# Attention in a hybrid decoder trunk: the products of probabilities and values issued in four bursts a group instead of eight calls in eight steps

## What is computed

```
q, k_c, v_c, k_s, v_s, k_w, v_w, g = split(rms_norm(x) @ w_in)     # 16 heads of 64, in 4 groups of 4 heads
o_c = softmax(q @ kc.T * scale, causal over blocks) @ vc           # compressed keys and values
o_s = softmax(q @ ks.T * scale, causal) @ vs                       # all 8 selected blocks of 64: the whole sequence
o_w = softmax(q @ kw.T * scale, causal) @ vw                       # a window of 512
o   = gates[0] * o_c + gates[1] * o_s + gates[2] * o_w
x   = x + o @ w_out
```

## Time and profile before

| what | before |
|---|---|
| median of three runs | 1432.88 us |
| the profiled execution's own time | 1434.92 us |
| its span on the core | 1433.1 us |
| TensorE busy | 1416.5 us, 99% |
| VectorE, ScalarE, GpSimd busy | 980.5, 699.4, 253.3 us |
| granted TensorE clock | 0.999 of full |
| the attention stream | from about 83 to 337 us of the span |

### The profile page before, as it was taken

The page is one execution under the profiler, slowest core; times in us unless marked ns, Lnnn a source line. Parts: engine busy times, 40 slices in busy tenths (PEclk is TensorE's granted clock), DMA queues, the critical chain, the costliest instruction groups (busy, mean ns, idle before and its releaser), DMA issues.

```text
span 1433.1 us, 18980 instructions
## 1 busy us (share of the span) xinstructions
PE 1416.5 (99%) x7282; PEld 1165.9 (81%) x7282; DVE 980.5 (68%) x1289; ACT 699.4 (49%) x1116; POOL 253.3 (18%) x278
## 2 busy tenths in 40 slices
PE   8999999999999999999999999999999999999999
PEld 7878888778888888888888877777788888888887
DVE  4797877875697888433487756779544988887231
ACT  5566666654445446422233357778324455455121
POOL 4324334101200000000100008776203000000000
PEclk9999999999999999999999999999999999999999
DMA  8200010311332332232232233332222432221322
GB/s 334 102 30 31 30 60 2 118 60 66 107 122 91 116 118 88 89 116 90 89 118 88 88 120 119 117 118 89 88 89 88 147 118 104 91 95 64 118 91 86
DMA packets 27461, 139.51 MB, mean 97 GB/s; under 512 B 2672, under 2 KB 3440, under 8 KB 17136
## 3 DMA queue, kind: packets, MB, share of 16 engines
q1 hardware_dynamic: 24640, 127.54, 25.5%
q10 hardware_dynamic: 2736, 10.81, 2.1%
HBM read 136.18 MB, written 2.16 MB: 97 GB/s over the span
## 4 chain that ended last, share of the span: by engine, by line
PE 91%; DVE 3%; ACT 3%; POOL 1%; issue 1%; DMA 0%; SPq 0%; ACTq 0%; DVEq 0%; POOLq 0%
PE ps L631 16%; PE ps L633 16%; PE ps L632 16%; PE ps L789 7%; PE ps L787 7%; PE ps L788 7%; PE ps L1045 5%; PE ps L1229 3%; PE ps L1023 2%; PE ps L1003 2%; PE ps L1281 1%; PE ps L768 1%; PE ps L912 1%; PE ps L947 1%; PE ps L948 1%
## 5 line engine op out<-in xcount | busy, mean ns | idle before, releaser
L1870 DVE TENSOR_TENSOR wl<-wraw,wh 128x2048 fp32r<-128x2048 f32 x77 | 176.6, 2294 | 159.6 <-ACT wh L1326 159.6
L1326 ACT ACTIVATE wh<-wraw 128x2048 fp32r<-128x2048 f32 x77 | 147.1, 1911 | 174.4 <-PE ps L633 172.0
L787 PE MATMUL ps<-wh,mix_hi 128*128 128x512 f32 x448 | 174.4, 389 | 0.0
L789 PE MATMUL ps<-wh,mix_lo 128*128 128x512 f32 x448 | 174.3, 389 | 0.0
L788 PE MATMUL ps<-wl,mix_hi 128*128 128x512 f32 x448 | 174.3, 389 | 0.0
L631 PE MATMUL ps<-xh,wh 128*128 128x512 f32 x384 | 152.4, 397 | 0.0
L633 PE MATMUL ps<-xh,wl 128*128 128x512 f32 x384 | 149.7, 390 | 0.0
L632 PE MATMUL ps<-xl,wh 128*128 128x512 f32 x384 | 149.6, 390 | 0.0
L631 PE MATMUL ps<-hidden_hi,wh 128*128 128x512 f32 x352 | 139.4, 396 | 0.0
L633 PE MATMUL ps<-hidden_hi,wl 128*128 128x512 f32 x352 | 137.1, 390 | 0.0
L632 PE MATMUL ps<-hidden_lo,wh 128*128 128x512 f32 x352 | 137.1, 389 | 0.0
(11 more groups left out here) (354 smaller groups left out, 3048.9 us busy)
## 6 DMA issues: line engine op xcount, KB each, us to landing
wraw<-wstream SPq DMA_DIRECT2D x95, 1024.0 KB, 4.9
wx<-wstream SPq DMA_DIRECT2D x16, 1024.0 KB, 6.8
rowc<-cum_rows ACTq DMA_DIRECT2D x16, 512.0 KB, 3.6
cw<-cw_in SPq DMA_DIRECT2D x1, 4096.0 KB, 14.0
xT<-xT_in SPq DMA_DIRECT2D x8, 256.0 KB, 6.6
part<-xT_in ACTq DMA_DIRECT2D x1, 2048.0 KB, 10.3
out<-xT SPq DMA_DIRECT2D x8, 256.0 KB, 6.4
wraw<-wstream SPq DMA_DIRECT2D x2, 512.0 KB, 8.8
```

What stands on the lines that cost most here:

```text
L787: mm(o, x, hi[:, :, w], start=start and k == 0, stop=False, skip_group_check=True)
L789: ins = mm(o, xl_, hi[:, :, w], start=False, stop=k == 3, skip_group_check=True)
L1326: A(wh[:, n % 2, :], wraw[:, n % 2, :], ACT.Copy).then_inc(hi_done, 1)
L1870: TTo(wl[:, s, :], wraw[:, s, :], wh[:, s, :].bitcast(F32), ALU.subtract).then_inc(lo_done, 1)
```

## The change

The table gives for each step a list of calls of `pv` instead of one. The calls for query tiles 0 and 1 of a pair follow each other directly, and so do those for tiles 2 and 3. For the first pair they stand in steps 10 and 12 (before: 10, 11, 12, 13), for the second in steps 15 and 19 (before: 15, 16, 17, 19). The other engines' programs are unchanged.

```diff
-            PV_AT = {10: (0, 0), 11: (0, 1), 12: (0, 2), 13: (0, 3), 15: (1, 0), 16: (1, 1), 17: (1, 2), 19: (1, 3)}
+            PV_AT = {10: ((0, 0), (0, 1)), 12: ((0, 2), (0, 3)), 15: ((1, 0), (1, 1)), 19: ((1, 2), (1, 3))}
...
                 if s in PV_AT and g < GROUPS:
-                    pv(g, *PV_AT[s])
+                    for pair, i in PV_AT[s]:
+                        pv(g, pair, i)
                 if s + 16 in PV_AT and g:
-                    pv(g - 1, *PV_AT[s + 16])
+                    for pair, i in PV_AT[s + 16]:
+                        pv(g - 1, pair, i)
```

## The result

Ten runs gave a median of 1436.59 us (1434.40 to 1438.23) against 1432.93 us in ten runs of the kernel before. The ratio is 1.0026, with a 95% interval of 1.0016 to 1.0036: slower by 3.7 us. The forecast was 1435.9 (1431.0 to 1438.6), with slower as the likeliest outcome.

The account below looks back on a forecast made before the run. TensorE was taken as the bound, 91% of the chain that ended last. Two groups at +0.79, +1.14 after group 2 and +0.33 in group 3 gave +3.05 us on the median 1432.88: 1435.9 us, range 1431.0 to 1438.6.

Parts of the forecast that it names:

- The drains: Change of width costs 0.35 us a burst, nothing inside a merged burst; 32 bursts become 16, saving 5.6 us.
- Rival (b): The boundary inside a merged burst keeps its 0.35 us: 5.6 us slower, 1438.5 us; chance 10%.
- Where it turns: Steps 12 to 18: pT(10) 1.61 us later, VectorE 1.14 later; stalls of 2.19 us in groups 0 and 1.
- The term of +0.79: Groups 0 and 1: each 0.79 us longer; without waits -1.40, so 2.19 us are stalls.
- rival (c): One more wait, at the projection of step 18 or 11: 0.3 to 0.5 us in three groups, 1437.3 us; 17%.
- The term of group 2, +1.14: After group 2 no projection fills TensorE and VectorE is busy, so its lateness stays: +1.14 us.
- Group 3: No split in step 13; -0.70 from steps 11 and 13, -0.5, +1.53 from step 19: +0.33 us.
- The middle of -0.98 and nothing: Group 3, step 17: 0.98 us early at best, bank 7 may take all of it; -0.5 taken.
- Rival (a): The drains are all that counts: 5.6 us come off, 1427.3 us; chance 8%.
- its halfway case: Stalls half the size (-5.6 + 4.3): 1431.6 us; chance 10%.

Follow-up runs that it names:

- Step 10 alone: Of the four merges only that of step 10 (first pair's tiles 0 and 1), the rest as in the kernel before; 1432.99 us, ratio 0.9995.
- the same program: The old order written in the new table's notation, the same instructions as the kernel before; 1434.17 us, ratio 1.0000.

## Why the prediction was right

**The drains**, 0.35 us a burst: right. Step 10 alone shows it three times over (0.35, 0.36, 0.35), and the boundary inside a burst costs nothing, the value taken. Rival (b) falls by the row at 181.55. The Trainium skill (TensorEngine Tiling (Array Packing), Key Properties) says that changing the tiling mode, not just the tile, drains TensorE. These traces agree: 0.35 us around a burst, nothing between two calls inside it. With 0.35 us for each of 16 bursts the drains alone would have given 5.6 us of gain.

**Where it turns**: right in mechanism and in size. pT(10) 1.60 late (1.61), maxima of step 14 by 1.06 (1.14), GpSimd's chain by 1.05 (1.14), 0.96 us of idle time printed before step 14's transposes, 1.11 by the starts (1.1 to 1.2), 0.64 before step 17's (over 0.5). The term of +0.79 was 0.07 too large in group 1, since VectorE's chain was given 1.14 instead of 1.06: without idle time the maxima start 0.08 before the printed end of the low part. In group 0 it was 0.15 too large, since GpSimd's chain ended another 0.24 earlier there (one of its rows, L2672, took 0.28 us instead of 0.59), so that only 0.41 us were idle before step 17's transposes; step 18 took 0.19 of this lead back (rival (c), below). The term of group 2, +1.14, was hit against the profile of before (+1.12); against the same program's 61.64 it is +1.31, with a fall of the clock in that stretch. That VectorE carries the lateness on there is borne out: from its maxima of step 14 to step 5 of group 3 its timeline shows one idle time, of 0.40 us (0.15 before).

**Group 3**: +0.15 instead of +0.33. Its merge of step 15 costs 0.94 as forecast (0.9). The middle of -0.98 and nothing, taken for what bank 7 gives back, was a guess, and its error is the largest of any term; by the sum -0.70 + 1.53 - x = 0.15 it is 0.68 instead of 0.5.

**Rival (a)**, the drains alone, doesn't hold, and neither does its halfway case. **Rival (c)**: between groups 0 and 1 step 18 took 3.35 us instead of the 3.16 it takes a group later, so the wait for the second chunk occurred once, for 0.2 us. It was no part of the loss that matters. Step 11 took 2.97 us, just the 4.41 of before less 1.44, so its projection didn't wait.

**The number.** The stream lost 2.64 to 2.88 us, against one or the other profile of the old order, where 3.05 was forecast; the medians differ by 3.66. The difference of 0.8 to 1.0 us lies in neither stream; it is within what the clock and the start do from run to run, and was not traced further. So the mechanism was right, while the closeness of 1436.59 to 1435.9 is partly luck: the forecast stream was 0.2 to 0.4 us too long, and 0.8 to 1.0 us that it knew nothing of came on top.

## What to carry to other kernels

When work moves from behind an instruction to ahead of it, look not at the moved work's own waits, but at what other engines did in its shadow: here a copy, a split and its low part, 0.60 + 1.90 + 2.29 us on two engines, lost their cover while the moved products had all they needed. Merging 64-wide products into one burst saves the change of width only in steps in which TensorE itself is the bound; where the next transposes wait for GpSimd, the same saving is nothing. Moving an operation to an earlier step helps only if its release comes early, too, and if it isn't put ahead of work that is wanted sooner: here the split began 2.7 us earlier and the stream stayed at 256.5.

## What the runs showed of the hardware

The clock falls to its lower level for short stretches, at places that differ from run to run. Behind group 2 the kernel after shows it where the kernel before doesn't (1.00 all through), after TensorE had stood 1.56 us and was busy for 1.97 of 3.50 us. Windows of the kernel after:

```profile
256.50:260.00 3.50, 1.97 (x19) 1.51 (x15) 3.40 (x5) 3.50 (x7) 3.27 (x4) 1.00 0.21 87
260.00:264.50 4.50, 4.31 (x20) 3.65 (x21) 4.33 (x11) 3.65 (x12) 2.85 (x6) 0.62 0.00 0
```

It seems to have cost little there: 62.95 us, against 62.80 in the kernel with the split in step 12 and 63.10 in that with only step 12 merged, whose clocks stayed up. These kernels differ in more than the clock, so its price isn't isolated; VectorE bounds that stretch. In the kernel with only step 15 merged, where pv(1,2) fell into it, the same event came with 1.25 us. A second place lies far behind the attention layer. The kernel before:

```profile
1004.00:1008.00 4.00, 2.22 (x18) 2.08 (x17) 3.73 (x7) 2.67 (x7) 2.72 (x4) 0.83 0.42 131
1008.00:1012.00 4.00, 4.00 (x15) 3.25 (x14) 3.90 (x5) 0.00 (x0) 4.00 (x4) 0.74 0.31 131
```

and the kernel with the change and the split in step 12:

```profile
1004.00:1008.00 4.00, 2.54 (x18) 1.94 (x16) 3.73 (x5) 3.83 (x11) 1.56 (x3) 1.00 0.20 29
1008.00:1012.00 4.00, 3.67 (x18) 3.13 (x19) 3.93 (x6) 0.00 (x0) 4.00 (x4) 1.00 0.56 233
```

TensorE waits about as long in both there (1.78 and 1.80 us for VectorE), but the clock falls in one only. From the end of the stream to the end of the program it is 1096.4 to 1097.0 us in the nine profiles in which it fell there, and 1095.0 to 1095.1 in the five in which it didn't: 1.4 us, as much as four bursts saved. Whether a changed stream shifts the odds of it was not tried. The start of the stream also moved, 81.2 to 82.7 us, for programs that are the same up to there.
